# Rebuilding the front part of a two-layer encoder kernel: activated vector, modulation loads, gate maps, norm statistics, out-projection

## What is computed

```python
cs = jax.nn.silu(c)
for l in range(2):
    mod = cs @ w_mod[l] + b_mod[l]                  # 6 x 1024 numbers
    sh1, sc1, g1, sh2, sc2, g2 = split(mod, 6)
    h = rmsnorm(x, norm_mix[l]) * (1 + sc1) + sh1
    x = x + g1 * (even_mixer if l == 0 else odd_mixer)(h)
    h = rmsnorm(x, norm_ffn[l]) * (1 + sc2) + sh2
    x = x + g2 * peer(h, w_q, sub_keys, u_tab, v_tab)
return rmsnorm(x, final_norm)
```

## Time and profile before

| | |
|---|---|
| median of 3 runs | 2241.05 us (2237.48 to 2243.5) |
| the profiled execution | 2241.37 us, its span 2239.6 us |
| TensorE matmul busy | 2083.1 us, 93% |
| VectorE busy | 1490.3 us, 67% |
| ScalarE busy | 1023.9 us, 46% |
| mean granted clock of TensorE | 0.961 |
| moved by DMA | 447.26 MB, mean 200 GB/s |

### The profile page before, as it was taken

The page is one execution under the profiler, slowest core; times in us unless marked ns, Lnnn a source line. Parts: engine busy times, 40 slices in busy tenths (PEclk is TensorE's granted clock), DMA queues, the critical chain, the costliest instruction groups (busy, mean ns, idle before and its releaser), DMA issues.

```text
span 2239.6 us, 43787 instructions
## 1 busy us (share of the span) xinstructions
PE 2083.1 (93%) x12524; PEld 1848.6 (83%) x12524; DVE 1490.3 (67%) x3680; ACT 1023.9 (46%) x2011; POOL 18.7 (1%) x39
## 2 busy tenths in 40 slices
PE   1887689999999999999998889999999999999997
PEld 0755579999999997777777567999999999888886
DVE  5443567875777667887784226785677766777776
ACT  1012124563555555555552222455455555555554
POOL 0000000000000000000000000000000000000000
PEclk7895799999999999999999999999999999999999
DMA  6961344873655688998881213576465568777774
GB/s 238 345 241 44 134 159 134 229 213 105 171 174 173 182 263 303 310 323 305 315 281 44 94 76 113 168 229 180 130 174 173 172 187 248 242 238 242 241 242 152
DMA packets 168453, 447.26 MB, mean 200 GB/s; under 512 B 18625, under 2 KB 85441, under 8 KB 163793
## 3 DMA queue, kind: packets, MB, share of 16 engines
q1 hardware_dynamic: 163472, 393.17, 56.4%
q0 software_dynamic: 4928, 53.45, 6.0%
HBM read 409.84 MB, written 36.70 MB: 199 GB/s over the span
## 4 chain that ended last, share of the span: by engine, by line
PE 88%; DVE 4%; DMA 4%; ACT 2%; issue 1%; SPq 0%; DVEq 0%; ACTq 0%
PE bank L409 87%; DMA raw<-in_v 2%; DMA wmod_ring<-in_w_mod 1%; ACT big L700 1%; PE bank L464 1%; DVE big L906 1%; DVE work L848 0%; DVE wmod_ring L864 0%; ACT hi L745 0%; DVE work L1174 0%; DVE big L970 0%; DVE a_lo L1087 0%; DVE raw L856 0%; DMA c_all<-in_c 0%; PE bank L629 0%
## 5 line engine op out<-in xcount | busy, mean ns | idle before, releaser
L1068 DVE TENSOR_TENSOR lo<-raw,hi 128x512 fp32r<-128x512 f32 x1024 | 702.1, 690 | 375.9 <-ACT hi L745 370.8
L745 ACT ACTIVATE hi<-raw 128x512 fp32r<-128x512 f32 x1024 | 641.8, 629 | 512.2 <-PE bank L409 479.6
L409 PE MATMUL bank<-x_hi,hi 128*128 128x256 f32 x2048 | 590.3, 288 | 1.6 <-ACT work L751 1.6
L409 PE MATMUL bank<-x_hi,lo 128*128 128x256 f32 x2048 | 579.3, 283 | 0.0
L409 PE MATMUL bank<-x_lo,hi 128*128 128x256 f32 x2048 | 579.1, 283 | 0.0
L409 PE MATMUL bank<-hi,a_hi 128*128 128x512 f32 x1024 | 402.9, 393 | 12.3 <-DVE a_lo L1087 9.0
L409 PE MATMUL bank<-lo,a_hi 128*128 128x512 f32 x1024 | 399.9, 391 | 0.0
L409 PE MATMUL bank<-hi,a_lo 128*128 128x512 f32 x1024 | 399.9, 390 | 0.0
L409 PEld LDWEIGHTS bank<-x_hi,hi 128*128 128x128 f32 x2048 | 392.3, 192 | 1.9 <-issue 1.9
L409 PEld LDWEIGHTS bank<-x_lo,hi 128*128 128x128 f32 x2048 | 392.7, 192 | 0.0
L409 PEld LDWEIGHTS bank<-x_hi,lo 128*128 128x128 f32 x2048 | 392.1, 191 | 0.0
(11 more groups left out here) (138 smaller groups left out, 1371.8 us busy)
## 6 DMA issues: line engine op xcount, KB each, us to landing
raw<-in_u SPq DMA_DIRECT2D x256, 512.0 KB, 4.0
raw<-in_v SPq DMA_DIRECT2D x256, 512.0 KB, 4.6
wmod_ring<-in_w_mod SPq DMA_DIRECT2D x96, 512.0 KB, 4.6
s_store<-work SPq DMA_DIRECT2D x256, 128.0 KB, 3.7
wmod_ring<-s_store SPq DMA_DIRECT2D x256, 128.0 KB, 3.6
big<-in_w_in POOLq DMA_DIRECT2D x10, 2048.0 KB, 12.0
big<-in_w_q POOLq DMA_DIRECT2D x16, 1024.0 KB, 6.1
big<-in_w_out POOLq DMA_DIRECT2D x2, 4096.0 KB, 13.1
```

The lines of the kernel that those rows point to most:

```text
L409: return nc.tensor.matmul(o, w, x, start=start, stop=stop, skip_group_check=free)
L745: f(hi[:, r % 2, c], raw[:, r, c], ACT.Copy).then_inc(s[l]["hi_done"], 1)
L1068: v.tensor_tensor(lo[:, r % 2, c], raw[:, r, c], hi[:, r % 2, c].bitcast(F32), ALU.subtract).then_inc(s[l]["lo_done"], 1)
```

## The change

- **Activated vector.** c is loaded as 128 x 8 instead of a row in every partition. Exp, reciprocal and product work on 128 x 8, and eight matmuls (a column spread out as weights, the identity moving) make the row for all partitions in two banks, which ACT and VectorE copy into `c_all`.
- **Modulation loads.** The first 11 tiles have a place each (the three ring buffers, six places in parts of `big` not yet filled, two in `raw`), tiles 11 to 15 reuse the first five, and tiles 16 to 47 rotate over six places in `big` where the first weight tiles have been used. x is issued behind tile 2, the parameters behind tile 7. The weight spans 0, 1 and 2 are released at tiles 2, 8 and 13, the gate weights first and without a wait. How many tiles VectorE works behind each odd unit is now a table, `LATE_BY`.
- **Gate maps.** The gate unit comes first in the projection. From unit 9 on a small matmul behind each unit spreads one head's `negcum` over all partitions in bank 5, 6 or 7; VectorE adds the column `cum_q` and the causal mask and keeps the map in `wmod_ring`. `map_scores` then has the two score matmuls alone, and `maxima` adds the kept map. Layer 1's first modulation loads wait until the eight maps are used.
- **Norm statistics.** The squares are now the weights and one column of ones moves, so the sums come out as one number for each token in a partition (128 x 2). Reciprocal, root and Newton step work on these, and two matmuls spread the result over the partitions into a bank, from which `norm_scale` reads. The sub-norm does the same with 128 x 8.
- **Out-projection.** The first four of the eight input tiles are multiplied for the first four output tiles as soon as attention's matmuls are over, before the sub-norm's sums; the other half follows behind `mix_ready`. Layer 1 does so too.

The core of the diff:

```diff
+FIRST_MODS = 11
+LATE_MODS = 6
...
+FOX_AT = 9
+LATE_BY = (0, 0, 1, 4, 7, 11, 15, 19, 23, 28, 32)
...
+def mod_slot(n):
+
+    if n < FIRST_MODS:
+        return n
+    if n < EARLY:
+        return n - FIRST_MODS
+    return FIRST_MODS + (n - EARLY) % LATE_MODS
...
+        first_mods = [wmod_ring[:, n] for n in range(MODS)]
+        first_mods += [big[:, V_AT + n * D:V_AT + (n + 1) * D] for n in range(TT)]
+        first_mods += [big[:, QK_AT + n * D:QK_AT + (n + 1) * D] for n in range(4)]
+        first_mods += [raw[:, 2 + n] for n in range(2)]
+        first_mods += [big[:, n * D:(n + 1) * D] for n in range(LATE_MODS)]
+        fox_maps = wmod_ring[:].rearrange("p a n -> p (a n)")
...
-            for r in range(MODS):
-                load_mod(r, r)
-            early = -(-EARLY // MODS)
-            for lo, hi in ((1, early), (early, NMOD // MODS)):
-                if lo == early:
-                    sp.wait_ge(s[0]["qk_ps"], 4)
-                with sp.Fori(lo, hi) as i:
-                    for r in range(MODS):
-                        sp.wait_ge(s[0]["mod_tile"], MODS * i + r - (MODS - 1))
-                        load_mod(MODS * i + r, r)
+            sp.dma_start(c8, a["c"]).then_inc(c_in, 16)
+            sp.dma_start(cst[:], a["consts"]).then_inc(const_in, 16)
+            for n in range(NMOD):
+                if n == 3:
+                    sp.dma_start(raw[:, 0:2].rearrange("p a n -> p (a n)"), a["x"]).then_inc(x_in, 16)
+                if n == 8:
+                    sp.dma_start(par[:, 0:408], a["params"]).then_inc(par_in, 16)
+                if EARLY <= n < EARLY + LATE_MODS:
+                    sp.wait_ge(s[0]["qk_ps"], gate_units(0) + n - EARLY + 1)
+                if mod_before(n) >= 0:
+                    sp.wait_ge(s[0]["mod_tile"], mod_before(n) + 1)
+                sp.dma_start(first_mods[mod_slot(n)], a["w_mod"][0, n]).then_inc(wm_in[mod_sem(n)], 16)
...
+                    sp.wait_ge(s[0]["map_max"], 16)
...
-                spans = q4 + [(at, v0), (v0, v1), (v1, v1 + GATE_COLS * KT)][:3 if l == 0 else 2]
-                for n, (b, e) in enumerate(spans):
-                    if l == 0 and n == 1:
-                        pool.wait_ge(s[0]["mod_tile"], EARLY - MODS)
+                spans = list(enumerate(q4 + [(at, v0), (v0, v1)]))
+                if l == 0:
+                    spans = [(6, (v1, v1 + GATE_COLS * KT))] + spans
+                for n, (b, e) in spans:
+                    if l == 0 and n < 3:
+                        pool.wait_ge(s[0]["mod_tile"], (2, 8, EARLY - 3)[n])
...
-                mm(bank[7 if i % 2 else 0][:, 0:T], ones, work[:, k % 4, :], k == 0, k == KT - 1).then_inc(norms["ss_ps"], 1)
+                for t in range(TT):
+                    last = mm(bank[7 if i % 2 else 0][:, t:t + 1], work[:, k % 4, t * P:(t + 1) * P], ones[:, 0:1], k == 0 and t == 0, k == KT - 1, True)
+                last.then_inc(norms["ss_ps"], 1)
+
+            def spread(i):
+
+                pe.wait_ge(norms["rms_ready"], i + 1)
+                for t in range(TT):
+                    last = mm(bank[6 if i % 2 else 3][:, t * P:(t + 1) * P], n_root[:, t:t + 1].to_broadcast([P, P]), ident)
+                last.then_inc(norms["rms_ps"], 1)
...
+                    if l == 0 and u == 4:
+                        pe.wait_ge(s[0]["cum_ready"], 1)
...
+                    if l == 0 and u == FOX_AT - 1:
+                        pe.wait_ge(s[0]["cum_ready"], 2)
+                        for t in range(TT):
+                            last = mm(bank[4][:, t * 8:(t + 1) * 8], cum[:, t * P:(t + 1) * P], ident[0:8, 0:8])
+                        last.then_inc(s[0]["fox_ps"], 1)
+                    if l == 0 and FOX_AT <= u < FOX_AT + 8:
+                        h = u - FOX_AT
+                        if h >= 3:
+                            pe.wait_ge(s[0]["fox_map"], h - 2)
+                        mm(bank[5 + h % 3][:, 0:T], selector(h), negcum).then_inc(s[0]["fox_ps"], 1)
...
-                    last = mm(c, qk[at:at + HD, tq, t * P:(t + 1) * P], qk[at:at + HD, tk, 0:w], True, not fox)
-                    if fox:
-                        mm(c, selector(i), negcum[:, 0:w], False, False)
-                        for u in range(t + 1):
-                            last = mm(c[:, u * P:(u + 1) * P], cum[:, t * P:(t + 1) * P], selector(i), False, u == t)
+                    last = mm(o[:, P * t:P * t + w], qk[at:at + HD, tq, t * P:(t + 1) * P], qk[at:at + HD, tk, 0:w])
...
+                def products(m, lo, hi):
+                    for k in range(lo, hi):
+                        last = mm(bank[m % 4][:, 0:T], wout[:, m, k, :], hT[:, k, :], k == 0, k == KT - 1)
+                    return last
+
+                pe.wait_ge(s[l]["av_copied"], KT // 2)
+                pe.wait_ge(wout_in, 16 * (l + 1))
+                for m in range(4):
+                    products(m, 0, KT // 2)
+                if l == 0:
+                    pe.wait_ge(s[0]["sub_sq"], 1)
+                    for c in range(KT):
+                        last = mm(bank[4][:, c:c + 1], big[:, c * P:(c + 1) * P], ones[:, 0:1])
+                    last.then_inc(s[0]["sub_ps"], 1)
+                    pe.wait_ge(s[0]["sub_y"], 1)
+                    for c in range(KT):
+                        last = mm(bank[5 + c // 4][:, (c % 4) * P:(c % 4 + 1) * P], sub_root[:, c:c + 1].to_broadcast([P, P]), ident)
+                    last.then_inc(s[0]["sub_wide"], 1)
                     pe.wait_ge(s[0]["mix_ready"], 1)
                 else:
                     pe.wait_ge(s[1]["av_copied"], KT)
-                pe.wait_ge(wout_in, 16 * (l + 1))
                 for m in range(KT):
                     if m >= 4:
                         pe.wait_ge(s[l]["x_mixed"], m - 3)
-                    for k in range(KT):
-                        last = mm(bank[m % 4][:, 0:T], wout[:, m, k, :], hT[:, k, :], k == 0, k == KT - 1)
-                    last.then_inc(s[l]["y_ps"], 1)
+                    products(m, KT // 2 if m < 4 else 0, KT).then_inc(s[l]["y_ps"], 1)
...
+            for k in range(KT):
+                last = mm(bank[1 + k // 4][:, (k % 4) * P:(k % 4 + 1) * P], silu8[:, k:k + 1].to_broadcast([P, P]), ident)
+                if k % 4 == 3:
+                    last.then_inc(c_ps, 1)
...
             def norm_root(i):
 
                 dve.wait_ge(norms["ss_ps"], KT * (i + 1))
-                link(v.tensor_scalar(work[:, 2, :], bank[7 if i % 2 else 0][:, 0:T], 1.0 / D, EPS, ALU.mult, ALU.add))
-                v.reciprocal(work[:, 0, :], work[:, 2, :]).then_inc(norms["rec_ready"], 1)
+                link(v.tensor_scalar(n_mean, bank[7 if i % 2 else 0][:, 0:TT], 1.0 / D, EPS, ALU.mult, ALU.add))
+                v.reciprocal(n_rec, n_mean).then_inc(norms["rec_ready"], 1)
                 dve.wait_ge(norms["root_ready"], i + 1)
-                root(work[:, 1, :], work[:, 2, :], work[:, 3, :])
+                root(n_root, n_mean, n_tmp).then_inc(norms["rms_ready"], 1)
 
             def norm_scale(i):
 
+                dve.wait_ge(norms["rms_ps"], i + 1)
                 for k in range(KT):
                     g = gain(4) if i == 4 else amp[i // 2][i % 2]
-                    v.scalar_tensor_tensor(out=hT[:, k, :], in0=xT[:, k, :], scalar=g[:, k:k + 1], in1=work[:, 1, :],
+                    v.scalar_tensor_tensor(out=hT[:, k, :], in0=xT[:, k, :], scalar=g[:, k:k + 1], in1=bank[6 if i % 2 else 3][:, 0:T],
                                            op0=ALU.mult, op1=ALU.mult).then_inc(norms["hat_ready"], 1)
 
...
+            def fox_map(h):
+
+                dve.wait_ge(s[0]["fox_ps"], h + 2)
+                for t in range(TT):
+                    w = P * (t + 1)
+                    c = slice(P * t, P * t + w)
+                    last = v.scalar_tensor_tensor(out=fox_maps[:, h * MAPW + P * t:h * MAPW + P * t + w], in0=bank[5 + h % 3][:, 0:w],
+                                                  scalar=cum_q[:, t * 8 + h:t * 8 + h + 1], in1=bias_map(0, 0)[:, c], op0=ALU.add, op1=ALU.add)
+                last.then_inc(s[0]["fox_map"], 1)
...
+                        modulate(0, EARLY + LATE_BY[u // 2], EARLY + LATE_BY[u // 2 + 1])
+                        if u == FOX_AT:
+                            dve.wait_ge(s[0]["fox_ps"], 1)
+                            link(v.tensor_copy(cum_q, bank[4][:, 0:16]))
+                            dve.wait_ge(bias_in, 16)
+                        for h in range(8):
+                            if u == FOX_AT + h + 1 + (h + 1) % 2:
+                                fox_map(h)
...
-                m, r, y, t = (big[:, 2048:3072], big[:, 0:1024], big[:, 1024:2048], big[:, 3072:4096])
+                link(v.tensor_scalar(sub_mean, bank[4][:, 0:KT], 1.0 / P, EPS, ALU.mult, ALU.add))
+                v.reciprocal(sub_rec, sub_mean).then_inc(s[0]["sub_rec"], 1)
+                dve.wait_ge(s[0]["sub_root"], 1)
+                root(sub_root, sub_mean, sub_tmp).then_inc(s[0]["sub_y"], 1)
```

(15 more changed lines are left out.)

177 lines of the change are left out of this document (99 added, 78 removed).

## The result

The changed kernel takes **2188.59 us** (median of 4 runs, 2186.42 to 2193.14) against 2242.28 for the kernel before (4 runs, 2237.48 to 2243.79): ratio **0.9767, 95% interval 0.9748 to 0.9786**, so 2.3% faster. The forecast was 2176 with a range of 2166 to 2192. The profiled execution took 2186.42 us, with a span of 2184.6.

What follows compares the result with a forecast made beforehand. TensorE was taken as 88% of the chain, mostly unchanged expert stages. Savings of 21.2 - 4.5 + 33.8 + 8.0 + 0.0 + 1.8 + 4.8 = 65.1 from 2241.3 gave 2176 us, range 2166 to 2192.

Steps and rivals of the forecast that it cites:

- Front: Loads up to the first projection matmul: it comes at 42.8 us instead of 64.03, 21.2 saved.
- The term of 1.8 us for the release at tile 13: Front: 1.8 us added because the last four spans and the bias are released with one to three tiles in flight.
- The forecast's own sign of being wrong: Front: the prediction is wrong if modulation tiles 13 to 15 come later than 45 us.
- The rival: Front: late weight spans starve the last two or three tiles, 9 us more, 2185 in all; chance 0.15.
- Projection: First projection matmul to first map: 99.5 us against 94.95, so 4.5 longer.
- The three stalls: Projection: selector matmuls 3, 5 and 7 wait for VectorE's maps, 1.8 us each, 5.4 in all.
- The end copy: End of the projection: ACT's 0.6 us copy is in the open, counted as 0.8 us.
- Attention: Layer 0's attention: first map to third exponentials 11.8 us instead of 45.6, the rest unchanged, 33.8 saved.
- the slower case: Projection: narrow gate unit and selectors hold it at 1.2 GHz, +87 us, 2263 in all; chance 0.02.
- Sub-norm: End of attention (E) to first mixed out-projection tile: E+15.5 us, 8.0 saved, bounds 14 to 20.
- Ring: Out-projection: three slots for layer 1's modulation tiles set the pace, so first mixed tile to norm stays 29.8 us.
- Norms: Norms 1 to 4: 1.8 us saved at each, less 0.3 in norms 2 and 4; 1.8 plus 4.8.

Runs made afterwards that it cites:

- e1: The changed kernel with the last four weight spans released after modulation tile 16 instead of 13: 2180.82 us, ratio 0.9726 to the kernel before.
- e11: The changed kernel unedited, one execution, on the same chip as e9: 2181.57 us, first projection matmul at 41.5.
- e2: The changed kernel with the gate maps made ahead of the late modulation tiles in the projection: 2178.75 us, ratio 0.9714 to the kernel before.
- e5: The changed kernel without gate maps, gate terms added to each head's scores by matmuls on 8 partitions: 2200.99 us, ratio 0.9838 to the kernel before.
- e3: The changed kernel with ten places instead of three for layer 1's modulation tiles in the out-projection: 2180.07 us, ratio 0.9725 to the kernel before.
- e8: The changed kernel with norm statistics over 128x256 again: 2188.29 us, ratio 0.9759 to the kernel before.
- e10: The changed kernel with norm statistics over 128x256 again and the last spans released at tile 16: 2185.55 us, ratio 0.9758 to the kernel before.
- e9: The changed kernel run again with nothing edited: 2185.12 us, ratio 0.9747 to the kernel before, first projection matmul at 51.0.

## Why the prediction was right in kind and 12.6 us short

The spans put 10.1 us of the miss into places; the other 2.5 are 2.2 us by which the median lies above the profiled execution, and rounding.

- **Front, 7.5 us: the term that was too small.** The volume and the rate held: with the starving gone the first matmul came at 41.4, where 41 was the bound without contention. The term of 1.8 us for the release at tile 13 measured 9 us in the late course and nothing in the early one. The forecast's own sign of being wrong, tiles 13 to 15 later than 45, was met by its tile 15 at 47.38. The rival had the right mechanism, and I gave it 0.15 because tiles would be "queued before the release". Being queued didn't protect them: of the three tiles in flight the first waited as it does in e1, and the other two, sharing by packets, came 5.5 and 6.2 us apart. An estimate from the packets: with turns one to one the tiles have a fifth of 0.43 MB/us, so 0.52 MB take 6.1 us. By the nine executions the rival deserved about 0.5. That its 2185 lies so near the profiled 2186.4 is partly luck: the front lost 7.5 of its 9, and other stages the rest. With the early course the one execution of e11 took 2181.57.
- **Projection, 2.2 us: mis-sized terms.** A selector was put at 0.45 and costs 0.82 in the pitch of a unit: 8 x 0.37 = 3.0 too little. The three stalls were 4.54, not 5.4. The end copy was in the open as said (0.69 idle), and the narrow gate unit cost nothing more: 8 x 0.82 + 0.6 for the small ones + 4.5 + 0.7 - 5.6 = 6.8, against 6.7 measured. e2 shows the stalls' cause.
- **Attention, right to 0.7 us**, and for the reason given: e5 brings the low clock back with the same 8-partition matmuls. So the slower case, with 0.02, was right to be small: with one selector to 16 dense matmuls the projection ran at 0.98. The 0.7 is one execution's: the same stage took 45.1 to 47.3 in the other traces with the maps, so 32 to 34.5 saved.
- **Sub-norm, right to 0.4 us, in part by luck.** Sums took 1.84 and not 2.4, the spread 2.05 about as said; the late half began at E + 13.0 instead of 13.6 and took 2.0 to its first result instead of 1.7. The forecast only mentioned that the half of four tiles may keep the clock up. In this execution it was up; in seven others with the half the spread ran wholly or mostly at the low level, and E + 15.06 became E + 16.4 to 18.6, inside the bounds of 14 to 20.
- **Ring, right:** 28.9 against 29.8 of pure carry-over, VectorE waiting for DMA, TensorE idle for 5.7 us; e3 takes it away.
- **Norms, right:** 1.6 to 1.8 each, norm 1 within 0.2 of its 1.8. e8 and e10 give the time back with the old statistics.
- **Expert stages, 2.4 us.** Layer 0's took 1.7 more, layer 1's 1.2 more, its out-projection 0.5 less. They are the same work; in the profiled executions here layer 0's took 892.4 to 898.8 us. I take it for scatter, but it was not tested.

## What to carry to other kernels

When a bulk transfer of large packets is released while small loads that the next stage needs are in flight, price it by the packets' ratio, for every load still in flight, and release it behind the last of them. Where two helpers' work for one consumer stands on one engine's queue, put first what the busy engine waits for. If one edit is to be judged to 5 us, compare stages in the traces, and the same stage in several: a front with two courses hid a 6.6 us loss here, and one code's way from attention to the first mixed tile took 15.06 us in one execution and 16.5 in another.

## What the runs showed of the chip that I had not expected

- One code, on one chip, has two courses of its front, 9.5 us apart (50.98 and 41.52). The release came at 32.29 in the late one and at 35.72 in the early one.
- TensorE's clock fell from 1.00 to 0.50 within continuous work, with the matmuls on 8 partitions (e5), and stayed there for more than 35 us.
- A selector on 8 partitions between dense matmuls costs 0.82 us of pitch, where a dense one with as many columns costs 0.43.
- A wait of 1.6 us in the projection was followed by 3.5 us at a mean clock of 0.59 in e1, and by none in the changed kernel's first profile.
- The same 16 spreading matmuls of the sub-norm, behind the same 7 us of dense ones, took 2.05 us in the changed kernel's first profile and 3.50 in e9, the same code.
